# The high part of the weight split moves from GpSimd to ScalarE in a two-block fp32 kernel

## The reference

```python
def first_block(x, ...):
    h = rmsnorm(x, norm_mix)
    zu, zv, zq, zf, zi, zo, g_a, g_b = split(h @ w_in)
    y_a = gmlp_branch(zu, zv, ...) @ w_up_a            # 512 wide
    y_b = hgrn2_branch(zq, zf, zi, zo, ...) @ w_up_b   # 8 heads, chunked recurrence
    x = x + (sigmoid(g_a) * y_a + sigmoid(g_b) * y_b) @ w_out
    x = x + square(relu(rmsnorm(x, norm_ffn) @ w_ff1)) @ w_ff2   # 4096 wide
    return rmsnorm(x, final_norm)

def second_block(x, c, ...):                            # two layers
    for l in range(2):
        mod = silu(c) @ w_ada[l] + b_ada[l]             # 1024 x 9216 matrix, one row
        # swiglu (2816 wide), then attention + pooling (l = 0) or short convolution (l = 1),
        # then swiglu again, each with its own modulated norm and gate
```

## Time and profile before

| | |
|---|---|
| median of 3 runs | 3047.17 us (3044.95 to 3049.79) |
| span of the profiled execution | 3042.2 us |
| PE busy | 2802.1 us, 92% |
| POOL busy | 2290.2 us, 75% |
| DVE busy | 1319.3 us, 43% |
| ACT busy | 475.0 us, 16% |
| chain that ended last | PE 73%, DVE 14%, issue 5%, POOL 4%, ACT 2% |

### The profile page before, as it was taken

How to read it: one execution, slowest core, us unless ns; L and a number is a source line. 1 busy time by engine, 2 the same in 40 slices (tenths; PEclk the granted TensorE clock), 3 DMA queues, 4 the chain that set the end, 5 groups by cost and what they waited for, 6 DMA issues and landing times.

```text
span 3042.2 us, 32794 instructions
## 1 busy us (share of the span) xinstructions
PE 2802.1 (92%) x12573; PEld 2285.8 (75%) x12573; DVE 1319.3 (43%) x1089; ACT 475.0 (16%) x615; POOL 2290.2 (75%) x994
## 2 busy tenths in 40 slices
PE   6988989988888869999896899998999989999998
PEld 5877868866676648888683788886888868778887
DVE  7887831277877882111507521115211155431112
ACT  3333321110100131000214210002100020120000
POOL 5644559878898958888764588887888878878886
PEclk8989999999898989999997999999999999999999
DMA  3211122257666723322220133322222222322222
GB/s 113 70 41 55 49 63 97 97 182 247 236 231 241 240 100 97 97 97 90 82 90 21 56 97 97 97 90 77 95 97 97 90 90 97 96 83 97 96 89 78
DMA packets 252087, 323.39 MB, mean 106 GB/s; under 512 B 5622, under 2 KB 242420, under 8 KB 243828
## 3 DMA queue, kind: packets, MB, share of 16 engines
q1 hardware_dynamic: 240740, 245.51, 25.0%
q10 hardware_dynamic: 11280, 76.94, 7.2%
HBM read 320.34 MB, written 2.10 MB: 106 GB/s over the span
## 4 chain that ended last, share of the span: by engine, by line
PE 73%; DVE 14%; issue 5%; POOL 4%; ACT 2%; DMA 1%; ACTq 0%; DVEq 0%; SPq 0%; POOLq 0%
PE po L651 19%; PE po L653 19%; PE po L652 19%; DVE ada_acc L1673 3%; PE po L630 3%; PE po L625 2%; PE po L626 2%; POOL w_lo L563 2%; POOL w_hi L560 2%; DVE nt L1374 1%; PE pm L771 1%; DMA ada_in<-in_w_ada_dram 1%; DVE ql L1537 1%; DVE kl L1541 1%; DVE stats L1355 1%
## 5 line engine op out<-in xcount | busy, mean ns | idle before, releaser
L560 POOL TENSOR_TENSOR w_hi<-w_raw,zero 128x1024 fp32r<-128x1024 f32 x472 | 1047.0, 2218 | 694.7 <-issue 267.5
L563 POOL TENSOR_TENSOR w_lo<-w_raw,w_hi 128x1024 fp32r<-128x1024 f32 x472 | 1227.0, 2600 | 37.0
L651 PE MATMUL po<-a_hi,w_hi 128*128 128x512 f32 x1792 | 702.0, 392 | 10.7 <-ACT ev L1230 5.7
L652 PE MATMUL po<-a_lo,w_hi 128*128 128x512 f32 x1792 | 699.0, 390 | 0.0
L653 PE MATMUL po<-a_hi,w_lo 128*128 128x512 f32 x1792 | 698.8, 390 | 0.0
L651 PE MATMUL po<-b_hi,w_hi 128*128 128x512 f32 x1152 | 464.7, 403 | 68.7 <-DVE b_lo L1708 38.2
L653 PE MATMUL po<-b_hi,w_lo 128*128 128x512 f32 x1152 | 459.2, 399 | 0.0
L652 PE MATMUL po<-b_lo,w_hi 128*128 128x512 f32 x1152 | 457.5, 397 | 0.0
L651 PEld LDWEIGHTS po<-a_hi,w_hi 128*128 128x128 f32 x1792 | 337.3, 188 | 84.9 <-issue 7.6
L653 PEld LDWEIGHTS po<-a_hi,w_lo 128*128 128x128 f32 x1792 | 337.5, 188 | 71.0
L652 PEld LDWEIGHTS po<-a_lo,w_hi 128*128 128x128 f32 x1792 | 337.5, 188 | 70.5 <-issue 0.7
(11 more groups left out here) (251 smaller groups left out, 2812.2 us busy)
## 6 DMA issues: line engine op xcount, KB each, us to landing
ada_in<-in_w_ada_dram ACTq DMA_DIRECT2D x64, 1152.0 KB, 5.3
w_raw<-in_ffn_wg_dram SPq DMA_DIRECT2D x44, 1024.0 KB, 5.3
w_raw<-in_ffn_wu_dram SPq DMA_DIRECT2D x44, 1024.0 KB, 5.3
w_raw<-in_w_ff_dram SPq DMA_DIRECT2D x32, 1024.0 KB, 5.5
w_raw<-in_ffn_wd_dram SPq DMA_DIRECT2D x32, 1024.0 KB, 5.2
w_raw<-in_w_in_dram SPq DMA_DIRECT2D x28, 1024.0 KB, 5.1
w_raw<-in_ffn_wd_dram SPq DMA_DIRECT2D x16, 768.0 KB, 4.7
w_raw<-in_w_in_c_dram SPq DMA_DIRECT2D x12, 1024.0 KB, 5.0
```

The costliest lines, as they stand in the source:

```text
L560: pool.tensor_tensor(w_hi[:, s, part], w_raw[:, s, part], zero8[:, 0:1].to_broadcast([P, UNIT // 2]), ALU.add).then_inc(split_done, 1)
L563: pool.tensor_tensor(w_lo[:, s, part], w_raw[:, s, part], w_hi[:, s, part].bitcast(F32), ALU.subtract).then_inc(split_done, 1)
L651: pe.matmul(o, wh, hi[:, k, :], start=(k == ks[0]), stop=False)
L652: pe.matmul(o, wh, lo[:, k, :], start=False, stop=False)
```

## The change

ACT makes `w_hi` with an ACTIVATE Copy whose output is fp32r; POOL makes only `w_lo`. The one semaphore of the split becomes two: `hi_done` (ACT, 2 for a unit) and `lo_done` (POOL, 2 for a unit). SP and PE wait for `lo_done`. POOL no longer waits for the landing or for PE; ACT does. Since ACT is in order, every `weight_hi` call has a place in its list, written by hand.

```diff
-                    sp.wait_ge(split_done, free * 2)
+                    sp.wait_ge(lo_done, free)
@@ gpsimd
-            def split(s, landed, free, before):
-                pool.wait_ge(raw_landed[s], landed)
-                if free is not None:
-                    pool.wait_ge(chunk_done, free)
-                pool.wait_ge(consts_ready, 14)
+            pool.wait_ge(consts_ready, 14)
+            def weight_lo(s, un):
                 for h in range(2):
                     part = slice(h * UNIT // 2, (h + 1) * UNIT // 2)
-                    pool.tensor_tensor(w_hi[:, s, part], w_raw[:, s, part],
-                                       zero8[:, 0:1].to_broadcast([P, UNIT // 2]), ALU.add).then_inc(split_done, 1)
-                    pool.wait_ge(split_done, before + (2 * h + 1))
+                    pool.wait_ge(hi_done, at(un, 2, h + 1))
                     pool.tensor_tensor(w_lo[:, s, part], w_raw[:, s, part], w_hi[:, s, part].bitcast(F32),
-                                       ALU.subtract).then_inc(split_done, 1)
+                                       ALU.subtract).then_inc(lo_done, 1)
@@ tensor (five places)
-                pe.wait_ge(split_done, at(un, 4, 2))
+                pe.wait_ge(lo_done, at(un, 2, 1))
@@ scalar
+            def weight_hi(un, halves=(0, 1), s=0):
+                for h in halves:
+                    part = slice(h * UNIT // 2, (h + 1) * UNIT // 2)
+                    if h == 0:
+                        act.wait_ge(raw_landed[s], at(un - s, 8, 16))
+                        if not (isinstance(un, int) and un < 2):
+                            act.wait_ge(chunk_done, at(un, 2, -2))
+                    act.activation(w_hi[:, s, part], w_raw[:, s, part], ACT.Copy).then_inc(hi_done, 1)
@@ norm: before squares 0, 2, 4; in the a_hi loop after k = 2 and 4 one half each
+                    if u0 is not None and k in (0, 2, 4):
+                        weight_hi(u0 + 2 + k // 2, s=(k // 2) % 2)
...
+                    weight_hi(u0 + 5, s=1)
...
@@ pair: after the evacuations and after the last gate step
+                        weight_hi(p * 4 + (U_HG + 6), s=0)
...
+                        weight_hi(p * 4 + (U_HG + 7), s=1)
...
+                weight_hi(p * 4 + (U_HG + 8), s=0)
...
+                    weight_hi(p * 4 + (U_HG + 9), s=1)
@@ mix loop, behind each sigmoid
+                    weight_hi(u0 + (2 + 2 * v), s=0)
+                    weight_hi(u0 + (3 + 2 * v), s=1)
@@ hidden_group of the first feed-forward
+                        weight_hi(un + 2, (0,), s=k % 2)
                         act.wait_ge(s_f_dve, ff_dve.after(f"hid{k}", g))
...
+                        weight_hi(un + 2, (1,), s=k % 2)
+                    elif not last:
+                        weight_hi(g * 8 + (U_FF + 2 + k), s=k % 2)
                     if k + 2 < DK:
                         load_ada(k + 2)
...
+            hidden_group(FFG - 1, last=True)
+            norm("final", U_FF + 8 * FFG - 4)
@@ loop of the second block's feed-forwards
+                        weight_hi(un + 2, s=0)
+                        weight_hi(un + 3, (0,), s=1)
...
+                        weight_hi(un + 3, (1,), s=1)
...
@@ attention block, behind the evacuations (the last ones stand before the exponential of lambda)
+                weight_hi(U_AB + v + 2, s=v % 2)
...
+                weight_hi(U_ABO + v, s=v)
```

More of the change, by code:

```diff
@@ L989, in done, with norm @@
                 act.wait_ge(chunk_done, at(un, 2, 2))
+            def weight_hi(un, halves=(0, 1), s=0):
[6 more added lines that the diff above has]
+                    act.activation(w_hi[:, s, part], w_raw[:, s, part], ACT.Copy).then_inc(hi_done, 1)
             def log_exp_table():
                 act.preload_act_table_set("natural_log_exp_and_others")
-            def norm(name):
+            def norm(name, u0=None):
                 na, nd = norm_act[name], norm_dve[name]
@@ L1003, in norm @@
                     act.activation(sq[:, k % 2, :], xT[:, k, :], ACT.Square).then_inc(s_n_act, na.one(f"sq{k}"))
+                if name == "mix":
+                    weight_hi(0, s=0)
                 act.wait_ge(s_n_pe, norm_pe[name].after("sum"))
@@ L1015, in norm @@
                         .then_inc(s_n_act, na.one(f"hi{k}"))
+                    if k in (2, 4):
+                        if name == "mix":
+                            weight_hi(1, (k // 2 - 1,), s=1)
+                        elif u0 is not None:
+                            weight_hi(u0 + 5, (k // 2 - 1,), s=1)
             log_exp_table()
@@ L1123, in pair @@
                             evac(1, p + 1)
-                    elif more:
-                        gate_step(p + 1, "lq")
-                        gate_step(p + 1, "rq")
+                    else:
+                        if more:
+                            gate_step(p + 1, "lq")
+                            gate_step(p + 1, "rq")
+                        weight_hi(p * 4 + (U_HG + 7), s=1)
                 act.wait_ge(s_h_dve, hg_dve.after(f"K{LV - 1}", p))
@@ L1212, in _, with hidden_group @@
                     .then_inc(s_m_act, mix_act.one("mh"))
-            norm("ffn")
-            with act.Fori(0, FFG) as g:
+            norm("ffn", U_OUT)
+            def hidden_group(g, last=False):
                 def load_ada(k):
@@ L1234, in _, with ffn @@
                                        ACT.Copy).then_inc(s_f_act, ff_act.one(f"hi{k}"))
+                        weight_hi(un + 2, (1,), s=k % 2)
+                    elif not last:
+                        weight_hi(g * 8 + (U_FF + 2 + k), s=k % 2)
                     if k + 2 < DK:
                         load_ada(k + 2)
-            norm("final")
-            def ffn(l, j):
-                norm(f"{l}{2 * j}")
+            with act.Fori(0, FFG - 1) as g:
+                hidden_group(g)
+            hidden_group(FFG - 1, last=True)
+            norm("final", U_FF + 8 * FFG - 4)
+            def ffn(l, j, before):
+                norm(f"{l}{2 * j}", before)
                 for g, n in enumerate(GROUPS):
@@ L1249, in ffn @@
                             .then_inc(s_w_act, ffn_act[l, j, g].one("hi"))
-            ffn(0, 0)
-            norm("01")
+                        weight_hi(un + 3, (1,), s=1)
+                    if g + 1 < len(GROUPS):
+                        for v in range(4):
+                            weight_hi(U_FFN[l, j, g] + n + v + 2, s=v % 2)
+                return U_FFN[l, j, len(GROUPS) - 1] + GROUPS[-1]
+            ffn_out = ffn(0, 0, None)
+            norm("01", ffn_out)
             act.dma_start(pool_m[:, :, :], pool_w_2[0].rearrange("g c d -> c g d")).then_inc(at_landed, 16)
@@ L1272, in _ @@
                     .then_inc(out_taken[v], 2)
+                weight_hi(U_AB + 6 + v, s=v)
             for v in range(2):
@@ L1326, in _ @@
                     pooled_hi(3)
-            ffn(0, 1)
-            ffn(1, 0)
-            norm("11")
+            ffn_out = ffn(0, 1, U_ABO)
+            ffn_out = ffn(1, 0, ffn_out)
+            norm("11", ffn_out)
             for it in range(PAIRS):
@@ L1335, in _ @@
                     .then_inc(out_taken[u0 % 2], 2)
+                weight_hi(u0 + 2, s=u0 % 2)
+                weight_hi(u0 + 3, s=(u0 + 1) % 2)
                 taken(act, u0 + 2)
@@ L1338, in _ @@
                     .then_inc(s_c_act, cv_act.one("hi"))
-            ffn(1, 1)
+                weight_hi(u0 + 4, s=u0 % 2)
+            ffn_out = ffn(1, 1, U_CO)
+            for v in range(2):
+                weight_hi(ffn_out + v + 2, s=v)
         @block.vector
```

27 lines of the change are left out of this document (17 added, 10 removed).

## The result

| | before | after |
|---|---|---|
| median | 3046.06 us (4 runs, 3038.68 to 3049.79) | 2955.07 us (4 runs, 2946.76 to 2955.88) |
| span of the profiled execution | 3042.2 us | 2953.1 us |
| DVE busy | 1319.3 us | 1146.1 us |
| ACT busy | 475.0 us | 928.2 us |
| POOL busy | 2290.2 us | 1251.5 us |

The ratio is 0.970, 95% interval 0.968 to 0.972: 3% faster. 2955 us is the number of rival A, so the first question is whether A's mechanism gave it.

What follows compares the result with a forecast made beforehand. PE was busy 92%, with gaps where DVE and POOL block each other. Terms 28 + 35.5 - 9 + 9 + 1 - 2 - 2.5 + 1.5 save 61.5 us: span 2981, time 2985 us, range 2965 to 3005.

Steps and rivals of the forecast that it cites:

- rival A: DVE's waits on POOL all but vanish; a first feed-forward turn becomes 11.6 us, total 2955 us; chance 0.18.
- ACT's copy, 1.06 us a half, hidden in most places: ACT rounds each half unit in 1.06 us, 500 us in all; mostly hidden behind PE.
- Rivals C and D: C: ScalarE late in each group, 3086 us, chance 0.11; D: ACT cannot copy in 1.06 us, no separate chance.
- The locks halve: DVE instructions are held up by POOL's splits less often; at boundaries with 6 blocks four hold-ups become two, 2.3 us.
- Rival B: DVE pays as often with `w_lo` alone; recurrence gains nothing, ring turns stay at 14.96 us, total 3029 us; chance 0.14.
- Recurrence, 28 us: Recurrence stage: PE's waits for DVE's `kl` shrink; 11.5 us in the third pair, 28 us over four pairs.
- Feed-forward, turn 14.05 us, 31 us in three groups: First feed-forward: evacuation-to-evacuation distance in a group's first half falls from 14.96 to 14.05 us; three groups gain 31 us.
- Last group, +9, with -4.5 in its first half: Fourth feed-forward group: late `w_hi` of k = 6 costs 9 us including the final norm; first half saves 4.5 us.
- Start of the kernel, 1.5 us: Kernel start: squares run without being held up by POOL, 1.5 us gained.
- Mix, attention, boundaries: Mix start loses 2 us, attention 2.5 us; feed-forward/norm boundaries with 6 blocks gain 9 us, the last feed-forward 1.
- Span to median, 5 us: Whole kernel: 5 us added between the profiled execution's span, 2981 us, and the median time, 2985 us.

Runs made afterwards that it cites:

- the additional sum: Against the kernel after, POOL executes one more 128x1024 TENSOR_TENSOR behind each of the 32 `w_lo` in the first feed-forward's ring: 2981.8 us, ratio 0.979.

## Why the prediction came out as it did

- *ACT's copy, 1.06 us a half, hidden in most places:* right (1050 ns). In the whole kernel PE waits 33.2 us for `w_lo`, 12.8 of it in the last group; before it waited 23.7 us for the split. Rivals C and D did not come.
- *The locks halve:* right, and shown by the additional sum. Rival B (the lock only changes its name) is refuted: the turn fell to 13.55 us, and `ql` of the recurrence went from 1294 to 993 ns, though `kl` stayed (1335 and 1380 ns), against what I had expected: its locks moved to places where PE did not wait for it (2.0 us in place of 25.4).
- *Recurrence, 28 us:* mis-sized, 40 us. The size of the long wait was right (8.8 us, measured 9.1: from 10.92 and 8.64 to 5.22 and 5.23 us between the products). The reason that I gave, that POOL has nothing to do until ScalarE has passed the query's gate, is more than is needed: with `w_hi` ahead of the gate PE did not wait there either. The two short ones were priced by the wait alone, 2.8 us; with the low clock behind them they were 5.2 us. The second pair gave 16.5 us (11.5), the fourth 6.2 (2.5).
- *Feed-forward, turn 14.05 us, 31 us in three groups:* 13.55 us and 40.3 us. Nine turns by half a microsecond of lock less are 4.5 us; the three second halves gave 7.0, 7.8 and 8.2 us in place of 6.1 each. There I had taken 11.2 us for a unit without gaps; in the kernel after it is 10.8. The unit that I took had no gap and a granted clock of 1.00, so why it was slower is open.
- *Last group, +9, with -4.5 in its first half:* right, 4.5 us in sum with the final norm, by the mechanism named.
- *Start of the kernel, 1.5 us:* the term that failed most in proportion, 8.2 us. I had put in about the size of one lock; five sums of squares stood behind five POOL instructions. DVE before, and then after:

```profile
21.38 2.23 DVE L1355 TENSOR_TENSOR stats<-stats,sq 128x512 f32<-128x512 f32 x1
```

```profile
19.01 0.68 DVE L1405 TENSOR_TENSOR stats<-stats,sq 128x512 f32<-128x512 f32 x1
```

- *Mix, attention, boundaries:* 3.8 us lost from the gMLP to the first ev (2); second block 8.8 us gained (7.5), which the 4 us by which the attention varies from trace to trace make a loose fit.
- *Span to median, 5 us:* 2 us here. In every execution listed for the kernel after, the time is 1.8 to 2.9 us above the span; my 5 us compared the span of one execution with the median of others.

Fewer locks on DVE, with some waits of PE added, was the forecast's mechanism, and the additional sums show it for the ring. The forecast failed in the size of three terms, all taken too small: start 6.7, recurrence 12.1 and feed-forward 9.3 us, together the 28 us between 61.5 and 89.1. Locks and the low clock behind PE's waits make up most of it by the rows; for part of the recurrence and for the slower unit the cause is open.

## What to carry to other kernels

Count how many POOL instructions that read SBUF stand beside DVE's chain, and charge one to each DVE instruction with two SBUF operands, however short (a COPY and a TENSOR_SCALAR paid here too); many short steps are the worst place for them. Moving half of a split to ScalarE pays where DVE is on the path, and then each ScalarE instruction needs its place: ahead of transfers that wait, behind the last rounding of a norm, never in a row ahead of short DVE steps. Price a wait of PE with the low clock behind it.

## What the runs showed of the hardware

- One more MEMSET of POOL (0.95 us) behind each `w_lo` of a turn costs the two `ada_acc` nothing, a COPY 0.8 us, a TENSOR_TENSOR 1.6 us.
- Steps with one SBUF tensor are held up too: TENSOR_SCALAR of 128x2 took 1.93 us beside a `w_lo` (0.17 us alone), and the copy of `stats` in the final norm 2.56 us against 0.42:

```profile
1024.38 2.56 DVE L1402 COPY stats<-sq 128x512 f32<-128x512 f32 x1
```

- DVE's eight scans in the third pair took 10.23 us beside four POOL instructions and 2.62 us without them.
